# Two layers of a hybrid mLSTM, state-space and attention block: projections of the next mLSTM head issued inside the scan of this one

## What is computed

```
def mlstm_mixer(...):            # 4 heads of width 128, two directions d
    q, k, v, log_i, log_f = projections of the normed tokens, k scaled by 128**-0.5
    for d in range(2):           # forward, backward (tokens flipped)
        hc, st = mlstm_chunk_scan(context tokens, zero state)
        hl, _  = mlstm_chunk_scan(latent tokens, st)
    h = h_d0 + h_d1
    return rms_norm(h, g) * sigmoid(ml_o)

# one step of the scan over a chunk of tokens, state (C, n, m)
    c_new = decay * cmat + einsum('bhs,bhsk,bhsv->bhkv', w, kc, vc)
    s   = einsum(qc, kc) * exp(dlog - m_t)
    num = einsum(s, vc) + g * einsum(qc, cmat);  den = sum(s) + g * qc.nvec
    h   = num / max(|den|, exp(-m_t))

# in each layer: mod = silu(c) @ w_mod[layer] + b_mod[layer]   (1024 x 6144)
#   x = x + gate * (mixers(norm(x)) @ w_out);  x = x + gate * relu(norm(x) @ w_up)**2 @ w_down
```

## Time and profile before

| | us |
|---|---|
| median of the 2 runs | 5159.66 (5091.46 and 5227.86) |
| the profiled execution | 5096.87 |
| its slowest core, first to last instruction | 5095.3 |
| fastest core of it | 5063.6 |
| TensorE busy | 3054.1 (60%) |
| VectorE busy | 2344.3 (46%) |
| ScalarE busy | 1674.2 (33%) |
| mean granted TensorE clock, all cores | 0.706 to 0.708 |

### The profile page before, as it was taken

One profiled execution on the slowest core, in us unless ns is written; L12 is line 12 of the kernel. 1 busy time (PEld: TensorE's weight loads), 2 busy tenths in 40 slices (PEclk: granted clock), 3 DMA queues, 4 the chain that ended last, 5 costly groups with the idle time before them and its releaser, 6 DMA issues.

```text
span 5095.3 us, 67340 instructions; the slowest of 8 cores (5063.6 to 5095.3 us)
## 1 busy us (share of the span) xinstructions
PE 3054.1 (60%) x17876; PEld 1672.6 (33%) x18028; DVE 2344.3 (46%) x6082; ACT 1674.2 (33%) x4466; POOL 95.7 (2%) x116
## 2 busy tenths in 40 slices
PE   2256664757334747687884566647572447558888
PEld 1133332535212323343441333325351223223333
DVE  0335555465745213454554344454656442135555
ACT  0434443535222522211114344435362135031111
POOL 1000000000000000000000000000000000000000
PEclk9566666656566558899996666666555655779999
DMA  9320001000000032233212200010000000322221
GB/s 156 109 26 9 1 1 21 1 1 1 1 13 1 1 100 42 34 50 50 42 17 80 26 9 1 1 21 1 1 1 1 13 1 1 99 33 34 34 34 67
DMA packets 114974, 144.54 MB, mean 28 GB/s; under 512 B 40880, under 2 KB 100400, under 8 KB 113584
## 3 DMA queue, kind: packets, MB, share of 16 engines
q0 software_dynamic: 106752, 82.32, 11.7%
q1 hardware_dynamic: 7856, 57.90, 3.2%
HBM read 195.26 MB, written 27.26 MB: 44 GB/s over the span
## 4 chain that ended last, share of the span: by engine, by line
PE 51%; DVE 16%; ACT 12%; issue 12%; DMA 7%; DVEq 1%; ACTq 1%; POOL 0%; POOLq 0%; SPq 0%
PE ps L280 49%; DMA W_wm<-w_mod 3%; DMA W_wo<-w_out 2%; PE psb L283 2%; ACT H_hT L291 1%; DVE X_raw L311 1%; ACT W_nsq L291 1%; DVE X_yacc L301 1%; DVE Y_act L301 1%; DVE W_ntmp L311 1%; DVE X_C L311 1%; ACT X_DTs L291 1%; ACT X_Cb L316 1%; DVE X_PTs L301 1%; ACT W_DTs L291 1%
## 5 line engine op out<-in xcount | busy, mean ns | idle before, releaser
L311 DVE SCALAR_TENSOR_TENSOR X_xT<-ps,C_modp,X_xT 128x512 f32<-128x512 f32 (+1 forms) x648 | 467.1, 721 | 403.4 <-PE ps L280 352.5
L280 PE MATMUL ps<-Y_act,Y_wd 128*128 128x512 bf16 (+1 forms) x2255 | 486.7, 371 | 147.8 <-DVE Y_act L301 145.1
L280 PE MATMUL ps<-H_hT,Y_wu 128*128 128x512 bf16 (+1 forms) x2262 | 486.5, 373 | 3.5 <-issue 1.5
L291 ACT ACTIVATE Y_rl<-ps 128x512 f32<-128x512 f32 (+1 forms) x288 | 164.8, 573 | 973.9 <-PE ps L280 944.5
L280 PEld LDWEIGHTS ps<-Y_act,Y_wd 128*128 128x128 bf16 x2304 | 221.9, 98 | 412.6 <-issue 184.9
L301 DVE TENSOR_TENSOR Y_act<-Y_rl 128x512 bf16<-128x512 f32 (+1 forms) x288 | 190.8, 662 | 335.9 <-ACT Y_rl L291 335.2
L280 PEld LDWEIGHTS ps<-H_hT,Y_wu 128*128 128x128 bf16 x2304 | 228.0, 99 | 250.1 <-issue 8.0
L280 PE MATMUL ps<-C_mnegb,C_cstb 128*128 128x128 bf16 x816 | 254.2, 312 | 0.0
L280 PE MATMUL ps<-X_GTl,C_cstb 72*128 72x128 bf16 x816 | 254.1, 312 | 0.0
L280 PE MATMUL ps<-X_GTh,C_cstb 72*128 72x128 bf16 x816 | 252.6, 310 | 0.0
L280 PE MATMUL ps<-Y_yT,W_wo 128*128 128x512 bf16 (+1 forms) x848 | 179.1, 373 | 105.3 <-DMA W_wo<-w_out 104.5
(11 more groups left out here) (186 smaller groups left out, 5057.5 us busy)
## 6 DMA issues: line engine op xcount, KB each, us to landing
W_wm<-w_mod POOLq DMA_DIRECT2D x24, 1024.0 KB, 12.3
xs_scratch<-X_xT SPq DMA_DIRECT2D x2, 9216.0 KB, 29.6
X_xT<-xs_scratch SPq DMA_DIRECT2D x2, 9216.0 KB, 32.4
Y_wu<-w_up POOLq DMA_DIRECT2D x16, 1024.0 KB, 9.6
Y_wd<-w_down POOLq DMA_DIRECT2D x16, 1024.0 KB, 9.1
W_xin<-x SPq DMA_DIRECT2D x16, 512.0 KB, 4.8
W_wq<-w_in POOLq DMA_DIRECT2D x32, 256.0 KB, 4.4
out<-W_xo SPq DMA_DIRECT2D x16, 512.0 KB, 2.7
```

The costliest lines, as they stand in the source:

```text
L280: S.op("pe", lambda e: e.matmul(out, lhsT=lhsT, rhs=rhs, start=start, stop=stop), R, W)
L291: S.op("act", lambda e: e.activation(out=out, in_=in_, func=func, **kw), R, W)
L311: S.op("dve", lambda e: e.scalar_tensor_tensor(out=out, in0=in0, scalar=scalar, in1=in1, op0=op0, op1=op1), R, W)
```

## The change

Two things are changed.

**mLSTM.** `qT`, `kT`, `ktok`, `vaug` and `osig` exist twice (`hbuf`); the second set lies in a part of `yT` that this stage doesn't use. The projection is a generator `ml_proj(h)` with 28 steps, one for each block of 8 matmuls with its evacuation. Head 0's is run alone. The scan of head h is run in turn with `ml_proj(h + 1)`: chain 0, chain 1, one block of projection. Projections use the banks ps4 and ps5 in turn. `dt_tile` writes into columns 260 to 387 of the bank that holds S and B.

**Modulation.** `mod_gen` issues the load of group fg + 1 ahead of the matmuls of group fg where there are two buffers, and layer 2's now has two (`wm1`, `wm1b`).

```diff
         mp = modp[l]
+        def ld(fg):
+            w_ = wm[fg % len(wm)]
+            DMA("pool", w_[:], wmod_d[l]....[:, :, fg * 512:(fg + 1) * 512], (), w_.b)
+
+        ld(0)
         for fg in range(12):
             w = wm[fg % len(wm)]
-            DMA("pool", w[:], wmod_d[l]....[:, :, fg * 512:(fg + 1) * 512], (), w.b)
+            if fg + 1 < 12 and len(wm) > 1:
+                ld(fg + 1)
+            elif fg > 0 and len(wm) == 1:
+                ld(fg)
             ps = P32()
...
-        qT = RX.alloc("qT", [128, NT], BF16)
...
+        hbuf = []
+        for si in range(2):
...
+            hbuf.append([al(f"qT{si}", ...), al(f"kT{si}", ...), al(f"ktok{si}", ...),
+                         al(f"vaug{si}", ...), al(f"osig{si}", ...)])
...
+        def ml_proj(h):
+            qT, kT, ktok, vaug, osig = hbuf[h % 2]
             w = wq[h % 2]
             for gq in range(4):
                 load_w(w, l, gq * 512 + h * 128, 128, gq * 128)
+            pc = 0
             for ti in tiles_all:
                 s0, n, j = TILES[ti]
-                ps = proj_feat(w, 0, ti)
+                ps = proj_feat(w, 0, ti, ps=ps32[4 + pc % 2]); pc += 1
                 CP("act", qT[:, s0:s0 + n], ps[:, 0:n], ps.b, qT.b)
-                ps = proj_feat(w, 128, ti)
+                yield
+                ps = proj_feat(w, 128, ti, ps=ps32[4 + pc % 2]); pc += 1
                 ACT(kT[:, s0:s0 + n], ps[:, 0:n], AF.Copy, ps.b, kT.b, scale=kscale)
+                yield
             for tb in range(NB):
-                ps = proj_tok(w, 128, 384, tb, tile_of(tb))
+                ps = proj_tok(w, 128, 384, tb, tile_of(tb), ps=ps32[4 + pc % 2]); pc += 1
                 ACT(ktok[:, tb, :], ps[:, 0:128], AF.Copy, ps.b, ktok.b, scale=kscale)
                 CP("dve", vaug[:, tb, 0:128], ps[:, 128:256], ps.b, vaug.b)
                 ACT(osig[:, tb, :], ps[:, 256:384], AF.Sigmoid, ps.b, osig.b)
+                yield
...
-                        dt_tile(gt, tb * 4 + h, d, tb, col, DTs[d], ps=bankD)
+                    dt_tile(gt, tb * 4 + h, d, tb, col, DTs[d], ps=bank1, c0=260)
...
+        run_rr([ml_proj(0)])
+        for h in range(4):
...
+            gl_ = [ml_chain(0, h, hbuf[h % 2]), ml_chain(1, h, hbuf[h % 2])]
+            if h + 1 < 4:
+                gl_.append(ml_proj(h + 1))
+            run_rr(gl_)
...
-            wm1 = [RW.alloc("wm1", [128, 8, 512], BF16)]
+            wm1 = [RW.alloc("wm1", [128, 8, 512], BF16), RY.alloc("wm1b", [128, 8, 512], BF16)]
```

More of the change, by code:

```diff
@@ L582, in layer, with al @@
         wq = [RW.alloc(f"wq{i}", [128, 8, 512], BF16) for i in range(2)]
-        qT = RX.alloc("qT", [128, NT], BF16)
-        kT = RX.alloc("kT", [128, NT], BF16)
-        ktok = RX.alloc("ktok", [128, NB, 128], BF16)
-        vaug = RX.alloc("vaug", [128, NB, 130], BF16)
-        osig = RX.alloc("osig", [128, NB, 128], F32)
+        hbuf = []
+        for si in range(2):
+            if si == 0:
+                al = lambda nm, shp, dt: RX.alloc(nm, shp, dt)
+            else:
+                yoff = [4 * NT * 2]
+                def al(nm, shp, dt):
+                    nbytes = (int(np.prod(shp[1:])) * (4 if dt == F32 else 2) + 31) // 32 * 32
+                    t_ = RY.alias(nm, shp, dt, yoff[0], [Buf(nm)])
+                    yoff[0] += nbytes
+                    assert yoff[0] <= 12 * NT * 2
+                    return t_
+            hbuf.append([al(f"qT{si}", [128, NT], BF16), al(f"kT{si}", [128, NT], BF16),
+                         al(f"ktok{si}", [128, NB, 128], BF16), al(f"vaug{si}", [128, NB, 130], BF16),
+                         al(f"osig{si}", [128, NB, 128], F32)])
         hacc = RX.alloc("hacc", [128, NB, 128], F32, nb=NB)
@@ L598, in layer @@
         ssq = RX.alloc("ssq", [128, NB], F32)
-        MSET("pool", vaug[:, :, 128:130], 1.0, vaug.b)
+        sqt = RX.alloc("sqt", [128, NB, 128], F32)
+        for si in range(2):
+            MSET("dve", hbuf[si][3][:, :, 128:130], 1.0, hbuf[si][3].b)
         kscale = 128.0 ** -0.5
-        for h in range(4):
+        orders = [scan_order(0), scan_order(1)]
+        hset = set()
+        def ml_proj(h):
+            qT, kT, ktok, vaug, osig = hbuf[h % 2]
             w = wq[h % 2]
@@ L687, in layer @@
                         gens.remove(g_)
-            if stop_after == 'ml_scan' and l == 0:
-                raise _Stop()
+        run_rr([ml_proj(0)])
+        for h in range(4):
+            osig = hbuf[h % 2][4]
+            for d in range(2):
+                MSET("dve", C32c[d][:], 0.0, C32c[d].b)
+                MSET("dve", Cbc[d][0][:], 0.0, Cbc[d][0].b)
+            hset.clear()
+            gl_ = [ml_chain(0, h, hbuf[h % 2]), ml_chain(1, h, hbuf[h % 2])]
+            if h + 1 < 4:
+                gl_.append(ml_proj(h + 1))
+            run_rr(gl_)
             b0 = out_blocks[0]
```

133 lines of the change are left out of this document (61 added, 72 removed).

## The result

| | before | after |
|---|---|---|
| median of the runs, us | 5098.19 (10 runs) | 5042.16 (11 runs) |
| fastest run, us | 5091.46 | 5036.56 |
| profiled execution, us | 5096.87 | 5066.82 |
| span of core 6 in it, us | 5095.3 | 5041.3 |

The ratio of after to before is 0.9895, 95% interval 0.9868 to 0.9921: 1.05% less, where the prediction had 5046 us and 1.0% less; the interval leaves out 1, so the gain is small and real. Some runs of every kernel are disturbed by a lower clock on one die; the ratios leave these out, and where a kernel had few others I give its fastest run. Core 1, the slowest in the profile after, has stretches at a granted clock of 0.81 in its last MLP, so I read core 6 of after, which has none, against core 6 of before.

The account below looks back on a forecast made before the run. No engine bounds the kernel throughout, so each stage was read alone. From 5096.9 us, -47.9 for modulation waits, -6.8 for slow clock behind them and +4 for the mLSTM gave 5046 us, range 5005 to 5090.

Parts of the forecast that it names:

- The modulation: MLP of layer 1: loading one call ahead removes TensorE's waits, -47.9 us, and slow-clock time behind them, -6.8 us.
- All four waits: MLP: TensorE's four waits for a load of `w_mod`, 47.9 us in all, were all to vanish.
- the half-clock term: MLP: TensorE's clock stays at 0.50 for a time after each long wait; without the waits, -6.8 us.
- "The waits for `Y_act` are 1.9 us each ... so none is given back": MLP: these waits, 79.0 us in 40, stay the same with or without a stall before the tile.
- Two banks: Projection: evacuation holds up TensorE and the first table load is no longer absorbed, +3.9 us for each projection.
- The joint stretch: mLSTM, next head's projection inside the scan: lasts 49.3 us, 9.0 more than the projection did.
- hole: Joint stretch: two Exps between Sigmoids need a table load each way, delaying the token blocks once, 2.8 us.
- If the clock fell in the stretch: Sign of being wrong: TensorE's clock was to stay at 1.00 in the joint stretch.
- The 5% rival: Joint stretch: TensorE's clock falls to half; if all 108 token blocks run so, +119 us, 5165 us; chance 5%.
- Layer 2 and head 3: mLSTM: a layer 2 stretch costs 9.0 us and saves 9.5; head 3's scan, following no projection, saves 1.9.
- How far the overlap reaches: mLSTM: the next projection's 28 steps fit into the first 1.9 of 18 scan iterations, saving 8.4 us a layer 1 head.
- the ring from the third iteration on: Scan: the loop over TensorE, ScalarE and VectorE was to keep its 4.17 us per iteration after the overlapped ones.

Follow-up runs that it names:

- run 1: The kernel before with only the modulation part, second buffer and load one group ahead: ratio to before 0.9893.
- run 3: The kernel before with its projections on the two banks ps4 and ps5 in turn, nothing overlapped: 5129.01 us, ratio to before 1.0056.
- runs 3 and 4: Besides run 3, the changed kernel with the output gate copied raw and its Sigmoid left out: fastest run 5001.68 us.

## Why the prediction was right, and where it was not

- *The modulation* (-54.7): right, shown by run 1 at -55.2. All four waits vanished, and the half-clock term with them.
- *"The waits for `Y_act` are 1.9 us each ... so none is given back"*: this step failed. They rose by 3.2 us in all (1.1 in the first tile, 0.28 to 0.36 in each of seven others), and two or three half-clock dips of 1.7 us each stand behind them: 7 us of the 54.7 were given back in the first MLP. I read the wait's mean of before and took it for a constant of the loop; it depends on which instruction meets an engine's pause. The second MLP, where I had no term, paid 3.9 back, since its four longer waits became one and its own two dips went. That this, the rest and layer 2's surplus add up to the forecast total within 1 us is luck.
- *Two banks* (+3.9 a projection): right, by head 0's projection and by run 3 (8 x 3.9 = 31). One sentence it starts from is a misreading: in the projection the others are not "nearly idle", ScalarE is busy 16.2 of the 40.3 us. The terms were worked out from ScalarE's rows all the same.
- *The joint stretch*: right in mechanism, and in layer 1 in size (48.6 against 49.3; loads, hole, 1.46 us, each at its place). The term left out is the clock dip, 1.5 to 3 us in 14 of 24 heads of layer 1 and 8 of 24 of layer 2; layer 1's surplus of 2.7 us over the forecast is no more than these. "If the clock fell in the stretch" was one of the prediction's own signs of being wrong, and it came. The 5% rival had seen the place and not the size: the clock falls there, for 3.4 us and not for all 108 blocks. The Trainium skill (*TensorE: Matmul & The Clock Gate*, section on a second HAM failure mode) has the clock swing under such short idles; the trace agrees that it can, with one swing in 22 of 48 stretches, and not that it governs the stretch: 0.93 and 0.97 are granted over the two shown, where the projection alone had 0.97.
- *Layer 2 and head 3*: mis-sized. A stretch of layer 2 without a dip costs 6.8 us over its projection and not 9.0 (47.5 against 40.7), and saves 10.3 and not 9.5: a head takes 126.2 us where it took 129.7. The hole of the Exps is there too (1.30 and 1.09 us on core 0). Its first two iterations have no Exps and no A, so less of the scan stands between the blocks than I had taken over from layer 1; that this is the whole reason is not shown. Head 3 saved 1.6 us in layer 1 and 3.3 in layer 2, where I had 1.9.
- *How far the overlap reaches* (2 of 18 iterations): right, and it is why the title's change moves nothing. Head periods of layer 1 changed from 134.6 to 134.9 where no dip falls into them, and to 137.8 on six cores for the one with head 2's projection, just over the 3 us that the prediction allowed. The gain that an engineer would have looked for went into the banks (+3.9 per projection) and the two table loads around the Exps, by runs 3 and 4.
- Table loads, 14 and 12 in the heads: as forecast. So is the ring from the third iteration on: 4.19 us in the median, as before, so `dt_tile` in the bank of S and B costs nothing.

## What to carry to other kernels

Before overlapping two pieces of work, count how many steps of the one the other has: a round robin that takes one step of each packs a short task into the first few iterations, and it saves only those iterations. The value of a filler is set by its place in every in-order queue it enters, not by the idle share of the engine: a block cost 0.3 to 0.8 us behind the last operation before a wait, 1.4 to 1.8 behind one whose successor is awaited, and blocks spread by count made an iteration 3 us longer. An operation that needs another table is first moved out of the stretch; that alone was worth 22 us here. And a wait measured in one kernel is not a constant of its loop: a change elsewhere, which gave ScalarE and VectorE other numbers of instructions, moved small pauses onto the waits of another stage and cost 7 us there.
